# Group norm of a gated linear-attention layer, moved into the scan and counted by tokens

## The chip, the cores and the metric

The kernel runs on one core of one Trainium2 chip. The time is the device time of one whole execution in microseconds (us). Three runs of the kernel before took 2664.95, 2672.15 and 2674.62 us; their median, 2672.15 us, is the time before.

The engines have short names below. PE is TensorE, and PEld its weight load. DVE is VectorE, ACT is ScalarE and POOL is GpSimd. SP is SyncE, which here only issues transfers. Each engine runs its own instructions in program order and waits at semaphores for the others.

## The reference, cut to what matters

The program is a stack of layers on 512 tokens with 1024 features, all in fp32. The change concerns only the end of one layer, an RWKV-7 mixer with 16 heads of 64 features:

```
y = _wkv7_scan(rh, decay, kh, vh, -kk, kk * ah)
mean = jnp.mean(y, axis=-1, keepdims=True)
var = jnp.mean(jnp.square(y - mean), axis=-1, keepdims=True)
y = (y - mean) * lax.rsqrt(var + GN_EPS)
y = y * ln_w.reshape(N_HEADS, HEAD_SIZE) + ln_b.reshape(N_HEADS, HEAD_SIZE)
bonus = jnp.sum(rh * kh * r_k, axis=-1, keepdims=True) * vh
out = ((y + bonus).reshape(bsz, seq, d).astype(h.dtype) * g) @ w_o
```

The scan carries a 64x64 state for each head. Its output y is linear in v. The norm is over the 64 features of a head, for each token. The gate g is `sigmoid(xg @ g1) @ g2`, and g2 (named gw2 in the kernel) and w_o are the two weight matrices that follow the scan.

## The kernel before, in words

**Layout.** Features lie on partitions: a tile [128, 512] is 128 features (two heads) by all 512 tokens, and `YT[:, f]` with f = 0 to 7 is the scan's output. `V[:, f]` is v in the same layout; it later holds the bonus term. `VT` is v with tokens on partitions.

**The scan.** The list `SCAN` is one order of steps, walked by PE, ACT and DVE alike. The tokens are cut into 4 chunks c of 128, each in two halves u of 64. A `group` (c, hf) inverts the in-chunk matrices of four pairs of heads; its steps are pa, px, pk, w and then p, q, t for each level. A `through` (c, u) carries the state over 64 tokens: `at` and `kt` (transposes), `ls` (L times state), `u` (T times that), `y` (the output: `ys` from the state, `yu` from U and v) and `state`. Up to three groups and one through are interleaved. `turn` transposes V into VT, and `bonus` makes the bonus term. After the last group only throughs are left, one behind another: this is called the tail here.

**After the scan.** The list `GROUP_NORM` interleaves four steps over the 8 feature tiles. A matmul with `bones` (ones within a head) spreads each head's sum to its 64 rows. DVE then centres YT. ACT squares it into `g4`, a second matmul with `bones` gives the variance, ACT takes its root, and DVE inverts the whole [128, 512] tile (line 1968), scales (1970) and adds ln_b and the bonus term (1973). Then come the dense products.

**Dense products.** `dense(name, ...)` walks the weight pieces. Each piece goes from `raw_` (4 slots, loaded by SP) into `WHs` by ACT (line 1063, "hi") and the rest into `WLs` by DVE (line 1571, "lo"), with 3 slots for the split pieces and a lookahead of 2 (`AHEAD`). A block of 128 output features takes three matmuls for each 128 input rows (lines 597 to 599). A "k" or "g" piece holds one k for several output blocks, so PE can start with k = 0 alone; an "m" piece holds all k of one block. The input of w_o is YT times the gate's product (DVE, line 1985). It is split by ACT (`oghi`, line 1358) and by DVE (even m, line 1988) or POOL (odd m, line 2277) into `oglo`.

**Banks.** PSUM has 8 banks, given out in turn by `Banks`; a taker waits until the bank's last contents were read ("free"). A held bank is skipped.

**Weights over the scan's memory.** The slots of raw_, WHs and WLs lie over the scan's buffers nb_. SP therefore loads the pieces from `HALT` on (the first of gw2) only when the groups have ended, and ACT splits them only after the last Y.

## Time and profile before

| | us |
|---|---|
| median of three runs | 2672.15 |
| the profiled execution, its own time | 2671.66 |
| its span, first to last instruction | 2669.8 |
| busy: PE, DVE, ACT, POOL | 2512.4, 1383.5, 899.7, 235.2 |
| the scan with what follows it, to the last matmul of w_o | about 805 to 1126.6 |

Starts and durations in the profile are in us from the span's start. A row of the timeline reads: start, duration, engine, line and operation, output<-input, shape, xcount, and in brackets the idle time of the engine just before it and what ended it. One fp32 matmul stands as two MATMUL records, a transpose as one, and a matmul on the split (fp32r) operands as one.

### The profile page before, as it was taken

To read this page: it belongs to the slowest core of one execution; us is meant where nothing else is said; L and a number is where in the kernel's file an instruction comes from. 1 tells how busy PE (TensorE), PEld (TensorE's weight loads), DVE (VectorE), ACT (ScalarE), POOL (GpSimd) and SP (SyncE) were. 2 spreads that over 40 slices of the span, in tenths; PEclk is the share of its full clock that TensorE was granted. 3 is DMA by queue.
4 is the path that set the end of the run, shared out by engine and by line. 5 is a ranking of instruction groups with operands and counts; after the bars stand their busy time and mean duration, and the time that the engine had idled before them with its cause. 6 is when DMAs were issued, how large, how long until landed. Compare 5 with 4: busy or idle time off the path is not lost.

```text
span 2669.8 us, 37239 instructions
## 1 busy us (share of the span) xinstructions
PE 2512.4 (94%) x15944; PEld 2037.9 (76%) x15944; DVE 1383.5 (52%) x2011; ACT 899.7 (34%) x1338; POOL 235.2 (9%) x199
## 2 busy tenths in 40 slices
PE   5999999989897895899999999999999999999998
PEld 4787888866676883688888888888766887788886
DVE  6774756647644547553344544433344654554433
ACT  3222413234642232242243332222245543332221
POOL 0000000002320000000000011100222000011100
PEclk9998999989999997999999999999999999999999
DMA  7563656612210001223332332233211331233332
GB/s 308 171 192 112 194 191 189 189 60 91 71 48 3 4 35 56 71 87 101 95 97 91 92 102 95 91 103 117 79 48 44 116 121 58 89 102 95 96 97 68
DMA packets 77796, 271.64 MB, mean 102 GB/s; under 512 B 8801, under 2 KB 9057, under 8 KB 76865
## 3 DMA queue, kind: packets, MB, share of 16 engines
q1 hardware_dynamic: 65808, 224.79, 26.3%
q0 software_dynamic: 11824, 44.49, 5.2%
q8 instruction: 126, 2.06, 0.3%
q14 instruction: 38, 0.30, 0.0%
HBM read 265.05 MB, written 4.19 MB: 101 GB/s over the span
## 4 chain that ended last, share of the span: by engine, by line
PE 85%; DVE 9%; ACT 3%; issue 2%; DMA 1%; SPq 0%; POOL 0%; DVEq 0%; ACTq 0%
PE ps L597 24%; PE ps L599 24%; PE ps L598 24%; PE ps L613 2%; DVE WLs L1571 2%; ACT WHs L1063 1%; DVE sqa L1968 1%; DMA raw<-in_cw_in_k 1%; PE ps L745 1%; DVE ada L1587 1%; PE ps L735 1%; PE ps L785 1%; PE ps L638 1%; PE ps L1013 1%; PE ps L1027 1%
## 5 line engine op out<-in xcount | busy, mean ns | idle before, releaser
L597 PE MATMUL ps<-HH,WHs 128*128 128x512 f32 x1728 | 695.7, 403 | 23.7 <-DVE HL L1657 11.5
L1571 DVE TENSOR_TENSOR WLs<-raw,WHs 128x1024 fp32r<-128x1024 f32 (+2 forms) x402 | 465.3, 1158 | 438.4 <-ACT WHs L1063 437.8
L599 PE MATMUL ps<-HH,WLs 128*128 128x512 f32 x1728 | 677.4, 392 | 0.0
L598 PE MATMUL ps<-HL,WHs 128*128 128x512 f32 x1728 | 676.9, 392 | 0.0
L1063 ACT ACTIVATE WHs<-raw 128x1024 fp32r<-128x1024 f32 (+2 forms) x420 | 415.6, 991 | 565.6 <-PE ps L599 562.5
L597 PEld LDWEIGHTS ps<-HH,WHs 128*128 128x128 f32 x1728 | 327.3, 189 | 102.3 <-issue 27.3
L599 PEld LDWEIGHTS ps<-HH,WLs 128*128 128x128 f32 x1728 | 326.7, 189 | 69.3
L598 PEld LDWEIGHTS ps<-HL,WHs 128*128 128x128 f32 x1728 | 327.5, 190 | 66.4 <-issue 2.2
L597 PE MATMUL ps<-HM,WHs 128*128 128x512 f32 x576 | 224.1, 389 | 0.0
L598 PE MATMUL ps<-HM,WHs 128*128 128x512 f32 x576 | 224.1, 389 | 0.0
L599 PE MATMUL ps<-HM,WLs 128*128 128x512 f32 x576 | 224.1, 389 | 0.0
L597 PE MATMUL ps<-HID,WHs 128*128 128x512 f32 x352 | 136.9, 389 | 0.0
L598 PE MATMUL ps<-HID,WHs 128*128 128x512 f32 x352 | 136.9, 389 | 0.0
L599 PE MATMUL ps<-HID,WLs 128*128 128x512 f32 x352 | 136.9, 389 | 0.0
L1108 ACT ACTIVATE sqa<-X 128x512 f32<-128x512 f32 x72 | 45.3, 631 | 238.2 <-DVE X L1628 234.8
L599 PEld LDWEIGHTS ps<-HM,WLs 128*128 128x128 f32 x576 | 108.1, 188 | 22.5
L597 PEld LDWEIGHTS ps<-HM,WHs 128*128 128x128 f32 x576 | 108.1, 188 | 22.5
L598 PEld LDWEIGHTS ps<-HM,WHs 128*128 128x128 f32 x576 | 108.1, 188 | 22.3
L2283 POOL TENSOR_TENSOR tmp<-tmp,sqa 128x512 f32<-128x512 f32 x24 | 41.3, 1722 | 868.8 <-ACT sqa L1392 868.8
L1587 DVE CUSTOM_DVE_ANT_0 ada<-ada,cbc 128x1024 f32<-128x1024 f32 x96 | 116.9, 1218 | 0.0
L597 PE MATMUL ps<-M0H,WHs 128*128 128x512 f32 x192 | 81.8, 426 | 29.5 <-DVE WLs L1571 17.6
L1733 DVE TENSOR_TENSOR tmp<-tmp 128x512 f32<-128x512 f32 x64 | 44.2, 691 | 102.6 <-ACT HM L1168 102.5
(371 smaller groups left out, 3222.0 us busy)
## 6 DMA issues: line engine op xcount, KB each, us to landing
ada<-in_adaw POOLq DMA_DIRECT2D x80, 512.0 KB, 4.8
raw<-in_f1gu_m SPq DMA_DIRECT2D x38, 512.0 KB, 3.6
raw<-in_f2gu_m SPq DMA_DIRECT2D x38, 512.0 KB, 3.6
raw<-in_mw_0b SPq DMA_DIRECT2D x32, 512.0 KB, 3.6
raw<-in_mw_1b SPq DMA_DIRECT2D x32, 512.0 KB, 3.6
raw<-in_w_in_m SPq DMA_DIRECT2D x18, 512.0 KB, 3.6
ada<-in_adaw SPq DMA_DIRECT2D x16, 512.0 KB, 15.3
raw<-in_cw_in_m SPq DMA_DIRECT2D x16, 512.0 KB, 3.7
```

What stands on the lines that cost most here:

```text
L597: pe.matmul(o[m], WHs[:, s, w], hi, start=k == 0, stop=False)
L598: pe.matmul(o[m], WHs[:, s, w], lo, start=False, stop=False)
L599: t = pe.matmul(o[m], WLs[:, s, w], hi, start=False, stop=k == DEPTH_K[name] - 1)
L613: t = pe.transpose(o[:, 128 * j:128 * j + 128], x(j), ident[:, :])
L638: t = pe.matmul(o, w[:, 128 * k:128 * k + 128], MW["g"][:, k], start=k == 0, stop=k == 7)
L735: t = pe.matmul(o[half(p), u, 32 * i:32 * i + 32], XT[half(u), n:n + 64], odd(T[half(u), m:m + 64], 2 << lv), start=True, stop=True)
L1063: act.activation(WHs[:, SLOT[v], 0:n], raw_[:, v % NRAW, 0:n], ACT.Copy).then_inc(*S.up("w_hi", ("hi", v)))
L1108: act.activation(sqt[f % 2][:, 0:n], src, ACT.Square).then_inc(*S.up("a_norm", ("sq", tag, f)))
L1571: dve.tensor_tensor(WLs[:, s, 0:n], raw_[:, v % NRAW, 0:n], WHs[:, s, 0:n].bitcast(F32), SUB).then_inc(*S.up("w_lo", ("lo", v)))
L1587: dve.tensor_tensor_reduce(tile, tile, cbc, 1.0, 0.0, MUL, ADD, mod[:, u:u + 1]).then_inc(*S.up("v_mod", ("dot", u)))
L1733: dve.tensor_tensor(x, x, x, MUL).then_inc(*S.up("v_evac", ("t2", name, m)))
L2283: pool.tensor_tensor(a_, a_, sqt[j % 2], MUL).then_inc(*S.up("g_ffn", ("ga", n, j)))
```

## The change

- v is centred per head before the scan: `turn` now multiplies V by `cen` = identity minus bones/64 instead of transposing it. Since y is linear in v, y comes out centred, and the mean step goes.
- The group norm is made per chunk of 128 tokens, in five steps placed in SCAN (chunks 0 to 2) or behind it (chunk 3). `squares`: ACT squares [128, 1024]. `sums`: 8 matmuls with the squares as weights and two columns of bones give a [128, 16] tile with tokens on partitions. `root` is made on that tile by ACT, and its reciprocal by DVE. `spread`: 16 matmuls of a broadcast column with the identity bring it back over two banks. `apply`: three DVE operations on [128, 1024] multiply by it, multiply by ln_w, and add V. ln_b is now added to V beforehand, by 8 ACT operations at the bonus steps (`V3`).
- gw2 is split in the tail (`gate_in`, `gate_weights`), and its 48 matmuls are issued as gate 0 to gate 7 between the steps of the last through and of chunk 3's norm. Each gate holds a bank. The two banks for chunk 3's spread are reserved ahead of gate 0.
- w_o becomes kind "g": eight pieces of one k and four blocks, then four "m" pieces. The products with the gate are made in a loop ahead of `dense("w_o")`. GHs and the state ST move to other places, and the slots are renumbered so that gw2 begins at slot 0.

```
+        ("gw2", "k", 8, 2), ("w_o", "g", 8, 8),
         ("mw1_1a", "e", 16, 8), ("mw2_1a", "m", 8, 16), ("mw1_1b", "m", 16, 8), ("mw2_1b", "m", 8, 16),
...
-EARLIER = {u: SPLIT[i - NSPLIT] for i, u in enumerate(SPLIT) if i >= NSPLIT}
+SLOT = {u: (i - SPLIT.index(HALT)) % NSPLIT for i, u in enumerate(SPLIT)}
+EARLIER = {u: SPLIT[i - NSPLIT] for i, u in enumerate(SPLIT) if i >= NSPLIT and not HALT <= u < HALT + NSPLIT}
 
...
+    for c in range(3):
+        part["norm", c] = [("norm", c, x) for x in ("squares", "sums", "root", "spread", "apply")]
+    part["gate_in"] = [("gate_in",)]
     groups = [("group", c, hf) for c in range(4) for hf in range(2)]
-    throughs = [("through", c, u) for c in range(4) for u in range(2)]
+    throughs = [("through", c, u) for c in range(4) for u in range(2)][:-1]
     at, ended, live, out = dict.fromkeys(part, 0), set(), ["turn", "bonus"], []
...
+                    live.append(("norm", x[1]))
+                if x == ("norm", 2):
+                    live.append("gate_in")
         if not live and not groups and throughs:
             live.append(throughs.pop(0))
-    return out
+    out += [("through", 3, 1, "ls"), ("gate_weights",), ("through", 3, 1, "u"), ("gate", 0), ("through", 3, 1, "y"), ("gate", 1)]
+    for i, x in enumerate(("squares", "sums", "root", "spread", "apply")):
+        out += [("norm", 3, x), ("gate", 2 + i)]
+    return out + [("gate", 7)]
 
...
-        g4 = [sqa[:, i] for i in range(4)]
...
+        gsq = sqa[:, 0:2].rearrange("p a (f t) -> p (a f) t", t=128)
+        pair = lambda c: YT[:, :, 128 * c:128 * c + 128]
...
+            def group_norm(c, part):
+                if part == "sums":
+                    o = bank("gsum", c)
+                    on.wait_ge(*S.at("gsq", c))
+                    for f in range(8):
+                        t = pe.matmul(o[:, 2 * f:2 * f + 2], gsq[:, f], bones[:, 0:128:64], start=True, stop=True)
+                    t.then_inc(*S.up("mm_scan", ("full", "gsum", c)))
+                if part == "spread":
+                    o = taken_two("gn", c) if c == 3 else bank_two("gn", c)
+                    on.wait_ge(*S.at("grec", c))
+                    for f in range(8):
+                        for p in range(2):
+                            n = 16 * c + 2 * f + p
+                            t = pe.matmul(o[half(p), f // 4, 128 * (f % 4):128 * (f % 4) + 128], ur[:, n:n + 1].to_broadcast([128, 64]),
+                                          ident[:, :], start=True, stop=True)
+                    t.then_inc(*S.up("mm_scan", ("full", "gn", c)))
+                    if c == 3:
+                        B.release(("gn", c), 2)
+
+            def gate_out(m):
+                u = FIRST["gw2"]
+                if m == 0:
+                    bank_two("gn", 3, hold=True)
+                o = bank("gw2", m, hold=True)
+                for k in range(2):
+                    on.wait_ge(*S.at("lo", u + k))
+                    on.wait_ge(*S.at("ghlo", k))
+                    s, w = SLOT[u + k], slice(128 * m, 128 * m + 128)
+                    pe.matmul(o, WHs[:, s, w], GHs[:, 0, k], start=k == 0, stop=False)
+                    pe.matmul(o, WHs[:, s, w], GHs[:, 1, k], start=False, stop=False)
+                    t = pe.matmul(o, WLs[:, s, w], GHs[:, 0, k], start=False, stop=k == 1)
+                t.then_inc(*S.up("mm_dense", ("full", "gw2", m), ("used", u), ("used", u + 1)))
+
...
                     for f in range(x[1], x[1] + 4):
                         o = bank("vt", f)
                         on.wait_ge(*S.at("V", f))
-                        turn(o, lambda j: V[:, f, 128 * j:128 * j + 128], [("full", "vt", f)], "mm_scan")
+
+                        for j in range(4):
+                            t = pe.matmul(o[:, 128 * j:128 * j + 128], V[:, f, 128 * j:128 * j + 128], cen[:, :], start=True, stop=True)
+                        t.then_inc(*S.up("mm_scan", ("full", "vt", f)))
                 if x[0] == "bonus":
...
 
-            for row in GROUP_NORM:
-                for f, step in row:
-                    if step == 0:
-                        on.wait_ge(*S.at("Y", 3, 1))
-                        o = bank("mean", f, hold=True)
-                        pe.matmul(o, bones[:, :], YT[:, f], start=True, stop=True).then_inc(*S.up("mm_scan", ("full", "mean", f)))
-                    if step == 1:
-                        B.release(("mean", f))
-                        on.wait_ge(*S.at("gs", f))
-                        o = bank("var", f, hold=True)
-                        pe.matmul(o, bones[:, :], g4[f % 4], start=True, stop=True).then_inc(*S.up("mm_scan", ("full", "var", f)))
-                    if step == 2:
-                        B.release(("var", f))
-
-            dense("gw2", lambda k: (GHs[:, 0, k], GHs[:, 1, k]), lambda k: ("ghlo", k))
...
                     if v == HALT:
-                        on.wait_ge(*S.at("Y", 3, 1))
+                        on.wait_ge(*S.at("full", "w", 3, 1, 1))
+                        on.wait_ge(*S.at("full", "u", 5, 1))
+                    if v == HALT + 2:
+                        on.wait_ge(*S.at("full", "u", 7, 1))
+                        on.wait_ge(*S.at("full", "ys", 7))
...
 
+            def group_norm(c, part):
+                if part == "squares":
+                    if c:
+                        on.wait_ge(*S.at("full", "gsum", c - 1))
+                    else:
+                        on.wait_ge(*S.at("full", "bonus", 7))
+                    on.wait_ge(*S.at("Y", c, 1))
+                    act.activation(gsq, pair(c), ACT.Square).then_inc(*S.up("a_scan", ("gsq", c)))
+                if part == "root":
+                    on.wait_ge(*S.at("full", "gsum", c))
+                    act.activation(ur[:, 16 * c:16 * c + 16], taken("gsum", c)[:, 0:16], ACT.Sqrt, scale=1.0 / 64,
+                                   bias=eps6[:, 1:2]).then_inc(*S.up("a_scan", ("gr", c), ("free", "gsum", c)))
+
             for x in SCAN:
+                if x[0] == "norm":
+                    group_norm(*x[1:])
+                if x == ("gate_in",):
+                    on.wait_ge(*S.at("Y", 2, 1))
+                    for j in range(2):
+                        on.wait_ge(*S.at("gk", j))
+                        act.activation(GHs[:, 0, j], GH[:, j], ACT.Copy).then_inc(*S.up("a_scan", ("ghhi", j)))
+                if x == ("gate_weights",):
+                    ahead(HALT - 1, len(WANT))
+                if x[0] == "bonus" and x[2] == 1:
+                    f = x[1]
+                    on.wait_ge(*S.at("V2", f))
+                    act.activation(V[:, f], V[:, f], ACT.Identity, bias=vc("ln_b", f)).then_inc(*S.up("a_scan", ("V3", f)))
                 if x[0] == "turn":
...
 
-            for n, row in enumerate(GROUP_NORM):
-                for f, step in row:
-                    if step == 1:
-                        on.wait_ge(*S.at("gc", f))
-                        if f >= 4:
-                            on.wait_ge(*S.at("gx", f - 4))
-                        act.activation(g4[f % 4], YT[:, f], ACT.Square).then_inc(*S.up("a_scan", ("gs", f)))
-                    if step == 2:
-                        on.wait_ge(*S.at("full", "var", f))
-                        act.activation(g4[f % 4], taken("var", f), ACT.Sqrt, scale=1.0 / 64,
-                                       bias=eps6[:, 1:2]).then_inc(*S.up("a_scan", ("gr", f), ("free", "var", f)))
-                if n == 4:
-                    on.wait_ge(*S.at("Y", 3, 1))
-                    for j in range(2):
-                        on.wait_ge(*S.at("gk", j))
-                        act.activation(GHs[:, 0, j], GH[:, j], ACT.Copy).then_inc(*S.up("a_scan", ("ghhi", j)))
-                if n == 6:
-                    ahead(HALT, len(WANT))
...
 
+            def group_norm(c, part):
+                if part == "root":
+                    u = ur[:, 16 * c:16 * c + 16]
+                    on.wait_ge(*S.at("gr", c))
+                    dve.reciprocal(u, u).then_inc(*S.up("v_scan", ("grec", c)))
+                if part == "apply":
+                    on.wait_ge(*S.at("full", "gn", c))
+                    x = pair(c)
+                    dve.tensor_tensor(x, x, taken_two("gn", c).rearrange("p a (f t) -> p (a f) t", t=128), MUL).then_inc(
+                        *S.up("v_scan", ("gx", c), ("free", "gn", c)))
+                    on.wait_ge(*S.at("gx", c))
+                    w = vc("ln_w", 0, 8).rearrange("p (f o) -> p f o", o=1).to_broadcast([128, 8, 128])
+                    dve.tensor_tensor(x, x, w, MUL).then_inc(*S.up("v_scan", ("gw", c)))
+                    on.wait_ge(*S.at("gw", c))
+                    on.wait_ge(*S.at("V3", 7))
+                    dve.tensor_tensor(x, x, V[:, :, 128 * c:128 * c + 128], ADD).then_inc(*S.up("v_scan", ("o", c)))
+
             for x in SCAN:
+                if x[0] == "norm":
+                    group_norm(*x[1:])
+                if x == ("gate_in",):
+                    for j in range(2):
+                        on.wait_ge(*S.at("ghhi", j))
+                        dve.tensor_tensor(GHs[:, 1, j], GH[:, j], GHs[:, 0, j].bitcast(F32), SUB).then_inc(*S.up("v_scan", ("ghlo", j)))
+                if x == ("gate_weights",):
+                    ahead(HALT - 1, len(WANT))
                 if x[0] == "bonus":
...
-                        dve.scalar_tensor_tensor(out=YT[:, f], in0=YT[:, f], scalar=vc("ln_b", f), in1=V[:, f], op0=ADD,
-                                                 op1=ADD).then_inc(*S.up("v_scan", ("o", f)))
-                if n == 4:
-                    for j in range(2):
-                        on.wait_ge(*S.at("ghhi", j))
-                        dve.tensor_tensor(GHs[:, 1, j], GH[:, j], GHs[:, 0, j].bitcast(F32), SUB).then_inc(*S.up("v_scan", ("ghlo", j)))
-                if n == 6:
-                    ahead(HALT, len(WANT))
-
...
+            ahead(FIRST["w_o"], len(WANT))
+            for m in range(8):
                 on.wait_ge(*S.at("full", "gw2", m))
-                on.wait_ge(*S.at("o", m))
+                on.wait_ge(*S.at("o", 3))
                 dve.tensor_tensor(YT[:, m], YT[:, m], taken("gw2", m), MUL).then_inc(*S.up("v_evac", ("og", m), ("free", "gw2", m)))
                 if m % 2 == 0:
                     on.wait_ge(*S.at("oghi", m))
                     dve.tensor_tensor(MX[0][1][:, m], YT[:, m], MX[0][0][:, m].bitcast(F32), SUB).then_inc(*S.up("v_in", ("oglo", m)))
-
-            dense("gw2", gate_out)
             dense("w_o", residual("w_o"))
```

## Rows read from the trace of the kernel before

**Rows 1.** Busy time by engine, three stretches (start:end, length, busy, granted clock, DMA)

```profile
940.00:960.00 20.00, 19.52 (x657) 18.85 (x658) 8.68 (x21) 7.39 (x14) 0.00 (x0) 1.00 0.02 4
...
1016.00:1063.00 47.00, 22.20 (x33) 7.15 (x33) 39.80 (x32) 14.89 (x21) 0.00 (x0) 0.71 0.22 78
1063.00:1126.70 63.70, 57.59 (x241) 44.41 (x239) 38.34 (x42) 18.79 (x26) 5.06 (x4) 1.00 0.22 70
```

**Rows 2.** Who waited for whom, 1016 to 1087 (total, times, longest)

```profile
PE ps L848 <- ACT sqa L1343: 24.8, 8, 7.9
```

**Rows 3.** Groups by line, 790 to 1130 (xcount | busy, mean ns | idle before)

```profile
L1968 DVE RECIPROCAL sqa<-sqa 128x512 f32<-128x512 f32 x8 | 26.7, 3343 | 0.0
...
L1571 DVE TENSOR_TENSOR WLs<-raw,WHs 128x1024 fp32r<-128x1024 f32 x13 | 16.0, 1240 | 5.8 <-ACT WHs L1063 5.8
...
L1063 ACT ACTIVATE WHs<-raw 128x1024 fp32r<-128x1024 f32 x12 | 12.3, 1043 | 5.0 <-PE ps L599 5.0
...
L1970 DVE SCALAR_TENSOR_TENSOR VY<-VY,vec,sqa 128x512 f32<-128x512 f32 x8 | 6.0, 752 | 0.3
```

**Rows 4.** Timeline, from the last Y to the end of w_o

```profile
1015.28 0.69 DVE L1926 TENSOR_TENSOR VY<-VY,ps 128x512 f32<-128x512 f32 x1 [2.88 <-PE ps L803]
...
1018.59 1.12 PE L848 MATMUL ps<-sqa,bones 128*128 128x512 f32 x2 [1.45 <-ACT sqa L1343]
...
1056.84 2.07 PE L848 MATMUL ps<-sqa,bones 128*128 128x512 f32 x2 [7.87 <-ACT sqa L1343]
...
1062.84 0.79 PE L597 MATMUL ps<-GHs,WHs 128*128 128x512 f32 x1
...
1074.50 0.47 PE L597 MATMUL ps<-M0H,WHs 128*128 128x512 f32 x1
...
1126.23 0.40 PE L599 MATMUL ps<-M0H,WLs 128*128 128x512 f32 x1
```

**Rows 5.** Timeline, the loop of gate products and their splits

```profile
1072.28 0.68 DVE L1985 TENSOR_TENSOR VY<-VY,ps 128x512 f32<-128x512 f32 x1
...
1074.27 1.28 DVE L1985 TENSOR_TENSOR VY<-VY,ps 128x512 f32<-128x512 f32 x2
...
1075.69 1.26 POOL L2277 TENSOR_TENSOR M0L<-VY,M0H 128x512 fp32r<-128x512 f32 x1 [288.95 <-ACT M0H L1358]
...
1076.24 1.26 DVE L1988 TENSOR_TENSOR M0L<-VY,M0H 128x512 fp32r<-128x512 f32 x1 [0.69 <-ACT M0H L1358]
...
1077.43 1.27 DVE L1985 TENSOR_TENSOR VY<-VY,ps 128x512 f32<-128x512 f32 x2
```

**Rows 6.** Timeline of the tail: chunk 3's first through

```profile
991.95 2.93 PE L613 MATMUL ps<-ident,KVA 128*128 128x128 f32 x16
...
994.80 1.76 PE L772 MATMUL ps<-nb,LR 64*64 64x64 f32 x32
...
997.35 2.02 PE L785 MATMUL ps<-nb,X 64*64 64x64 f32 x31 [0.79 <-DVE nb L1917]
...
1002.43 0.69 DVE L1926 TENSOR_TENSOR VY<-VY,ps 128x512 f32<-128x512 f32 x1 [2.28 <-PE ps L803]
...
1004.30 0.69 DVE L1934 TENSOR_TENSOR nb<-nb,ps 128x512 f32<-128x512 f32 x1 [1.18 <-PE ps L816]
...
1008.00 3.35 PE L785 MATMUL ps<-nb,X 64*64 64x64 f32 x29 [0.78 <-DVE nb L1917]
```

**Rows 7.** Timeline: the nearest relatives of `spread`, of `sums`, and a transpose

```profile
751.72 1.09 PE L676 MATMUL ps<-ident,ur 128*64 128x128 f32 x16
...
756.77 3.40 PE L668 MATMUL ps<-bones,sqa 128*128 128x2 f32 x29
...
804.92 1.91 PE L613 MATMUL ps<-ident,KVA 128*128 128x128 f32 x16
```

**Rows 8.** Table loads of ACT, by line, 900 to 1400

```profile
L1346 ACT ACT_TABLE_LOAD x1 | 1.3, 1283 | 0.0
```

**Rows 9.** Transfers, 975 to 1130 (KB each, median us from issue to landing)

```profile
X<-x_keep SPq DMA_DIRECT2D x1, 2048.0 KB, 8.0
```

66 lines of the change are left out of this document (23 added, 43 removed), and 1 row of the table PROJ.

## The prediction

> **What bounds the kernel now.** I read the page first: PE is busy for 94% of the span, so the kernel gains only where PE stands idle, or where its work is taken away. The busy time by stretches shows the one weak place near the change. From 1016 to 1063 PE is busy for 22.2 of 47 us, at a granted clock of 0.71, while DVE is busy for 39.8 [rows 1]. This is the group norm. Before it, at 940 to 960, PE is busy for 19.5 of 20 us; after it the clock is 1.00 again [rows 1]. The waits name what PE lacked: in eight matmuls it waited 24.8 us for ACT's squares, 7.9 us at the longest [rows 2]. ACT in turn stood behind DVE. The groups by line show why: eight reciprocals of [128, 512] cost 3.34 us each, 26.7 us, with no idle time before them, and the scale and the ln_b step add two times 0.75 for each tile [rows 3]. So DVE sets the order of the 47 us. The timeline gives the frame of my sum: the last Y ends at 1015.97, the gate's product begins at 1062.84 and w_o at 1074.50, and the last matmul of w_o ends at 1126.63 [rows 4]. What follows w_o is the same in both kernels, so the end of w_o carries the difference.
>
> **Rates.** 48 gate matmuls take 1074.50 - 1062.84 = 11.66 us [rows 4]; the first is slow, the others come every 0.235 us. Six (one gate) cost 1.4, twelve (one k of four blocks) 2.8, 24 (one block of w_o) 5.6. The nearest row to `spread` has 8 such matmuls (16 records) in 1.09 us [rows 7], so 16 cost 2.1. The nearest to `sums` has 29 records in 3.40, or 0.117 each [rows 7]; 16 records cost 1.85. DVE on [128, 1024] takes 1.24 and ACT 1.04 [rows 3]; I halve these for 512 columns: 0.6 to 0.65.
>
> **Work added before the last Y.**
>
> Centring v. A transpose costs 1.91/16 = 0.12 [rows 7]. A product with `cen` is two records of 0.117, or 0.23. For 32 of them that is 3.8 us more; a DVE wait can hide part of the second half. I take 3.2 (bounds 1 and 7). A rule of the Trainium skill speaks more strongly against this edit: "TensorE: Matmul & The Clock Gate", Terms, has fp32 transposes four times faster through the transpose mode. By it a product would cost 0.48 and the edit 11.5 us; the rows, where ordinary fp32 products of that weight size come every 0.23, don't bear that out.
>
> Norms 0 and 1 lie among the groups. PE is nearly full there [rows 1], so its share, 1.85 + 2.1 = 3.95 each, goes on the path: 7.9. DVE's `apply` is 3 x 1.24 = 3.7 and blocks masks and additions queued behind it. DVE is busy for only 8.7 of 20 us [rows 1], and three groups are in flight, so I count 0.8 for each norm beside that. Sum 9.5; lower bound 5, if PE's share fills idle time; upper bound 24, if nothing is hidden (12 each: 3.95 + 3.7, 1.1 for the squares, 1.3 for a table load, some 2 of semaphores). The square root's table load, 1.28 us once [rows 8], moves into norm 0. It runs on ACT beside p3's matmuls and costs nothing; uncovered, it would be 1.3. The eight ln_b additions on ACT (5 us) wait for DVE's V2, but ACT's next moves need PE steps that come later: nothing, 5 if uncovered.
>
> Norm 2 lies in the tail, where one through's steps wait for each other. `sums` stands between at and kt: 1.85 on the path. `spread` stands ahead of u. Before, PE waited there 0.8 us for DVE [rows 6], so 2.1 costs 1.3. `apply` (3.7) stands on DVE ahead of the Y addition; DVE idles 2.28 and then 1.18 there [rows 6], 3.46 in all, so 0.25 stays. Together 3.0 after a little overlap (3.4 at most). The split of GH and of gw2's two pieces (DVE 1.3 + 2.5) lies beside ls (1.76) and u (3.35) [rows 6] and costs nothing; without u's slow clock, 1. `sums` and `spread` wait for nobody late.
>
> Gate 0 stands between u and the last y: 1.4. All further gates lie beside waits.
>
> The last Y moves from 1015.97 by 3.2 + 9.5 + 3.0 + 1.4 = 17.1 to 1033.1. Call it t0.
>
> **From t0 to w_o.** Gate 1 begins before t0, gate 2 follows, and both end at t0 + 2.05, after ACT's square (1.1). Sums to 3.9, gate 3 to 5.3, gate 4 to 6.7, while root and reciprocal of 16 columns run beside them; spread to 8.8. DVE's first multiplication ends at 10.15. Only that frees the two banks of the spread, and following the bank turns gate 5 takes the first of them. So gates 5 to 7 run from 10.2 to 14.4. Now a wait that the order adds: ahead of its loop of gate products DVE walks the weights of w_o to the third piece, and the second's slot is gw2's, free when gate 7 ends. ACT splits at 15.1, DVE at 15.8 and once more at 16.45. All eight gate products, and apply before them, are queued in front of or behind that wait, so the loop begins at t0 + 16.45.
>
> **The loop and w_o.** The loop keeps its pace: the first product at 1072.28, pairs at 1074.27 and 1077.43, so 2.0 for the first and 3.15 for each pair; DVE's 1.26 lies beside POOL's 1.26 [rows 5]. Eight products end 12.1 after its start. PE can't use k = 0 at once. By the bank turns, block 0 of w_o takes the bank of gate 3 and block 1 that of gate 4, freed at about 5.8 and 6.4. Three k steps then end at 5.85 + 8.4 = 14.25. The fourth piece of w_o is split only when ACT and DVE have left the loop: 12.1 + 0.7 + 0.6 + 0.65 = 14.1. Both limits agree; five more k steps (14.0) and four blocks (22.4) give 50.65. Before, this part was 1126.63 - 1072.28 = 54.4 from the loop's start, so kind "g" itself brings only some 4 us.
>
> PE stands idle for 7.9 us ahead of w_o. After an idle of 7.87 two records took 2.07, against 1.12 after 1.45, and u in the tail took 3.35 instead of 2.02 [rows 4, 6]. That is the lower clock level, 1.2 GHz, for a while. I add 1.5 (0 to 4).
>
> X's return (8.0 us for 2 MB [rows 9]) is issued at t0, and its first reader comes some 45 us later; w_o's third and fourth piece are queued on SP behind it, and are needed at t0 + 15: nothing, 3 if they are late. The added table `cen` is one 64 KB transfer at the start: nothing.
>
> Sum: w_o ends at 1033.1 + 16.45 + 50.65 + 1.5 = 1101.7 instead of 1126.6, 24.9 us earlier. Against the profiled execution's own 2671.66, which is 0.5 from the median of the runs, that is 2646.8; I say 2647.
>
> **Rivals.**
>
> More is gained (0.10). The norms' PE work fills idle slots (5 instead of 9.5), centring costs 1, and the clock stays up in tail and w_o (3): about 34 to 37 us, 2636. Against it: PE is full where norm 1 lies.
>
> The scan pays for the norms (0.15). An in-order engine that waits for a norm holds up three groups. DVE's reciprocal waits for ACT's root, which is queued behind ACT's moves and a table load; masks stand behind it. At 12 us for each norm, three cost 36 instead of 12.5: 23.5 more, 2670, within 0.5% of before. The 47 us would then only have been moved. For it: the tail has no other work to hide behind. Against it: DVE is less than half busy in the scan.
>
> PE falls to its lower level in w_o (0.05), the slower side. The gate's product, broken into pieces by waits, leaves PE cold, and waits for banks and pieces keep it there. 192 matmuls at twice 0.235 cost 45 more: 2692. It decides from 38 us on, so from most of w_o. Against it: before, w_o began with waits for POOL as well, and the clock there was 1.00 [rows 1]. The Trainium skill ("TensorE: Matmul & The Clock Gate", A second HAM failure mode: psum-queue depth-cycling) tells of micro-idles between groups of matmuls that re-throttle the engine; no row here shows that for dense products.
>
> **Chances and range.** The forecast has 0.70 (its own range 2639 to 2657). A measurement of this kernel can tell about 0.5%, 13.4 us, from no change. Faster by more: 0.70 + 0.10 = 0.80; within: 0.15; slower: 0.05. The range 2634 to 2661 takes in the better rival and the bounds of centring, clock and part of the norms' upper bound.
>
> **What would show it.** The last Y near 1033; no reciprocal of 3.34 us; `sums` near 1.85 and `spread` near 2.1 us; the two-bank multiplication near 1.25; gates 5 to 7 behind that multiplication; DVE waiting about 2 us for ACT's split after gate 7; a first w_o matmul about 22 us after the last Y; the last one near 1102. The prediction is wrong if the groups' stretch grows by over 20 us, if the tail's through stalls at the spread, or if w_o's k steps take over 3 us.

## The result, and the profile after

| us | before | after |
|---|---|---|
| median (7 runs each) | 2672.15 | 2649.41 |
| lowest and highest run | 2663.83, 2674.62 | 2641.63, 2657.82 |
| the profiled execution, its own time | 2671.66 | 2657.82 |
| its span | 2669.8 | 2656.0 |

The ratio is 0.993, with a 95% interval of 0.9909 to 0.9952: 13 to 24 us faster, by the ratio 18.7; by the two medians it is 22.7. The forecast was 2647, or 24.9 us faster. The profiled execution of after is the slowest of its seven runs, so a second profile of the same kernel (e1_again below: 2652.62 us) stands beside it where a size matters.

The page of the changed kernel begins:

```profile
span 2656.0 us, 37616 instructions
...
PE 2524.0 (95%) x16136; PEld 2064.7 (78%) x16136; DVE 1355.3 (51%) x1999; ACT 901.1 (34%) x1342; POOL 235.6 (9%) x200
```

DVE lost 28 us of work and PE gained 12. The groups by line, 790 to 1130, show the new norm's parts (xcount | busy, mean ns | idle before):

```profile
L827 PE MATMUL ps<-ident,ur 128*64 128x128 f32 x128 | 9.3, 307 | 0.0
...
L819 PE MATMUL ps<-bones,sqa 128*128 128x2 f32 x64 | 9.1, 273 | 0.0
...
L858 PE MATMUL ps<-cen,KVA 128*128 128x128 f32 x64 | 7.6, 277 | 0.0
...
L1980 DVE TENSOR_TENSOR VY<-VY,ps 128x1024 f32<-128x1024 f32 x4 | 4.8, 1211 | 4.2 <-PE ps L827 4.2
...
L1976 DVE RECIPROCAL ur<-ur 128x16 f32<-128x16 f32 x4 | 1.0, 252 | 19.0 <-ACT ur L1363 19.0
```

The reciprocals fell from 26.7 us [rows 3] to 1.0. For all four chunks, sums take 9.1 us of PE (L819), the spread 9.3 (L827). Centring takes 7.6 (L858), or 0.24 for each of the 32 products.

Now the milestones, each read from the timeline. The scan is counted from the start of DVE's last `LR<-ps,X` evacuation ahead of it, so that what an execution lost earlier doesn't enter.

| us | before | after | e1_again |
|---|---|---|---|
| start of the scan, to the end of the last Y | 210.9 | 238.3 | 232.0 |
| last Y to the loop of gate products | 56.3 | 16.3 | 16.3 |
| loop's start to the end of w_o | 54.4 | 53.2 | 53.4 |
| start of the scan to the end of w_o | 321.5 | 307.9 | 301.7 |
| end of w_o, absolute | 1126.6 | 1108.8 | 1103.5 |

Behind the last Y 41 us went, and 21 to 27 came back ahead of it. The timeline of after, first inside the scan (chunk 1's norm), then in the tail, then behind the last Y (1038.47):

```profile
975.87 0.25 DVE L1976 RECIPROCAL ur<-ur 128x16 f32<-128x16 f32 x1 [4.12 <-ACT ur L1363]
...
976.96 1.97 PE L827 MATMUL ps<-ident,ur 128*64 128x128 f32 x32
...
980.97 0.68 DVE L1952 COPY sqa<-ps 64x512 f32<-64x512 f32 x1 [3.01 <-PE ps L780]
...
982.37 1.21 DVE L1980 TENSOR_TENSOR VY<-VY,ps 128x1024 f32<-128x1024 f32 x1
...
983.63 1.25 PE L788 MATMUL ps<-LR,nb 64*64 64x64 f32 x32 [1.79 <-DVE VY L1980]
...
1008.72 3.41 PE L819 MATMUL ps<-bones,sqa 128*128 128x2 f32 x16
...
1032.33 0.79 PE L842 MATMUL ps<-GHs,WHs 128*128 128x512 f32 x1
...
1038.47 0.69 DVE L1958 TENSOR_TENSOR VY<-VY,ps 128x512 f32<-128x512 f32 x1 [5.34 <-PE ps L798]
...
1041.22 1.84 PE L819 MATMUL ps<-bones,sqa 128*128 128x2 f32 x16
...
1045.88 1.97 PE L827 MATMUL ps<-ident,ur 128*64 128x128 f32 x32
...
1049.17 0.50 PE L842 MATMUL ps<-GHs,WHs 128*128 128x512 f32 x1 [1.32 <-DVE VY L1980]
...
1054.30 1.29 DVE L1603 TENSOR_TENSOR WLs<-raw,WHs 128x512 fp32r<-128x512 f32 x2 [2.07 <-ACT WHs L1089]
1055.51 0.68 DVE L2020 TENSOR_TENSOR VY<-VY,ps 128x512 f32<-128x512 f32 x1
...
1061.43 0.77 PE L592 MATMUL ps<-M0H,WHs 128*128 128x512 f32 x1 [7.88 <-DVE VY L2020]
```

The reader is to see two things. Everything behind 1038.47 comes as forecast: sums 1.84, spread 1.97, gate 5 at 1049.17 only when DVE's two-bank multiplication is done, DVE's 2.07 us wait at L1603, the loop at 1055.51, and w_o at 1061.43 after 7.88 us of idle PE. Inside the scan, at 983.63, PE waits 1.79 us for that same multiplication. The forecast has no such wait. The list of waits, 805 to 1040, has it twice (total, times, longest):

```profile
PE ps L788 <- DVE VY L1980: 1.8, 1, 1.8
PE ps L608 <- DVE VY L1980: 1.8, 1, 1.8
```

What waits is a taker of one of the spread's two banks: a transpose (L608) in chunk 0's norm, and the output `ys` (L788) in chunk 1's. The spread ends at 978.9, but DVE multiplies only at 982.37: between them stand PE's u (L780), the copy of it (980.97) and four additions of a group, which the common order puts ahead of `apply`. The banks' turn had come round by then.

Busy time by stretches of after (start:end, length, busy, granted clock, DMA):

```profile
965.00:1004.00 39.00, 37.21 (x943) 35.65 (x942) 16.77 (x35) 10.08 (x18) 0.00 (x0) 0.82 0.09 31
...
982.00:984.00 2.00, 0.37 (x12) 0.38 (x14) 1.97 (x5) 0.00 (x0) 0.00 (x0) 1.00 0.03 8
984.00:1000.00 16.00, 16.00 (x348) 15.50 (x343) 6.98 (x13) 2.62 (x5) 0.00 (x0) 0.57 0.01 2
1000.00:1004.00 4.00, 4.00 (x129) 3.95 (x127) 1.03 (x2) 1.53 (x3) 0.00 (x0) 1.00 0.82 281
```

Behind the wait the granted clock is 0.57 for 16 us in which PE is never idle: mostly the lower of its two levels, 1.2 GHz. In the tail it is low for a while too: sums take 3.41 instead of 1.84 (1008.72).

What the lower level costs the scan as a whole is read from the whole stretch, from the start of the scan to the end of the last Y: after, then e3_no_norms (below), the same kernel without the norms of chunks 0 to 2.

```profile
800.84:1039.16 238.32, 209.82 (x5705) 191.68 (x5704) 117.86 (x245) 71.25 (x122) 0.00 (x0) 0.89 0.03 10
```

```profile
802.57:1013.34 210.77, 186.19 (x5561) 169.64 (x5560) 107.06 (x233) 65.79 (x115) 0.00 (x0) 0.94 0.03 11
```

PE is idle for 28.5 us in the first and 24.6 in the second. The three norms' own 144 records come to 11.4 us at full clock (1.84 and 1.97 for each norm), but PE is busy for 23.6 us more. The rest of that is the same work done at the lower level.

### The profile page after: what moved, and what is told of

It is laid out like the page before. It is cut to its first block, busy times and chain, and to the rows that moved or that the text cites. A ratio compares the mean times of both kernels' runs of the same rounds, so it can differ in the third digit from the quotient of the medians.

```text
span 2656.0 us, 37616 instructions
## 1 busy us (share of the span) xinstructions
PE 2524.0 (95%) x16136; PEld 2064.7 (78%) x16136; DVE 1355.3 (51%) x1999; ACT 901.1 (34%) x1342; POOL 235.6 (9%) x200
## 3 DMA queue, kind: packets, MB, share of 16 engines
q1 hardware_dynamic: 66384, 224.79, 25.8%
## 4 chain that ended last, share of the span: by engine, by line
PE 87%; DVE 8%; ACT 3%; issue 1%; DMA 1%; SPq 0%; DVEq 0%; ACTq 0%
PE ps L592 24%; PE ps L593 24%; PE ps L594 24%; PE ps L608 2%; DVE WLs L1603 2%; ACT WHs L1089 1%; PE ps L730 1%; DMA raw<-in_cw_in_k 1%; DVE ada L1619 1%; PE ps L780 1%; PE ps L740 1%; PE ps L633 1%; PE ps L1035 1%; PE ps L1049 1%; PE ps L697 0%
## 5 line engine op out<-in xcount | busy, mean ns | idle before, releaser
L592 PE MATMUL ps<-HH,WHs 128*128 128x512 f32 x1728 | 696.2, 403 | 23.6 <-DVE HL L1689 11.3
L1603 DVE TENSOR_TENSOR WLs<-raw,WHs 128x1024 fp32r<-128x1024 f32 (+2 forms) x406 | 466.4, 1149 | 445.8 <-ACT WHs L1089 445.1
L592 PEld LDWEIGHTS ps<-HH,WHs 128*128 128x128 f32 x1728 | 327.5, 190 | 101.9 <-issue 26.7
L594 PEld LDWEIGHTS ps<-HH,WLs 128*128 128x128 f32 x1728 | 327.2, 189 | 69.8
```

The costliest lines, as they stand in the source:

```text
L592: pe.matmul(o[m], WHs[:, s, w], hi, start=k == 0, stop=False)
L594: t = pe.matmul(o[m], WLs[:, s, w], hi, start=False, stop=k == DEPTH_K[name] - 1)
L1603: dve.tensor_tensor(WLs[:, s, 0:n], raw_[:, v % NRAW, 0:n], WHs[:, s, 0:n].bitcast(F32), SUB).then_inc(*S.up("w_lo", ("lo", v)))
```

## The experiments

e1 to e4 ran on one chip, e5 to e8 on a second, g1 to g4 on a third, each time beside the kernel before. Ratios are to the kernel before on that chip. "Scan" is the first row of the table above, "behind" is the last Y to the end of w_o. "Idle" is what PE did not fill of the scan, and "clock" the granted clock over it, both from one profile by stretches.

| | median us | ratio, interval | scan | idle | clock | behind |
|---|---|---|---|---|---|---|
| e1_again | 2653.32 | 0.9942, 0.9926 to 0.9957 | 232.0 | 26.7 | 0.90 | 69.7 |
| e2_transposed_v | 2648.90 | 0.9928, 0.9910 to 0.9947 | 229.5 | 30.1 | 0.92 | 69.7 |
| e3_no_norms | 2629.54 | 0.9850, 0.9833 to 0.9868 | 210.8 | 24.6 | 0.94 | 69.7 |
| e4_norms_behind | 2645.94 | 0.9916, 0.9892 to 0.9941 | 204.4 | 24.2 | 0.97 | 89.1 |
| e5_gates_behind | 2650.46 | 0.9932, 0.9915 to 0.9950 | 228.6 | 29.3 | 0.92 | 74.6 |
| e6_w_o_blocks | 2653.06 | 0.9936, 0.9921 to 0.9952 | 232.9 | 25.7 | 0.90 | 72.2 |
| e7_weights_late | 2649.58 | 0.9922, 0.9905 to 0.9940 | 233.6 | 27.7 | 0.91 | 68.8 |
| e8_late_banks | 2647.71 | 0.9919, 0.9902 to 0.9936 | 227.7 | 25.8 | 0.92 | 66.5 |
| g1_multiply_early | 2647.65 | 0.9909, 0.9884 to 0.9933 | 226.0 | 26.6 | 0.93 | 69.8 |
| g2_small_apply | 2646.21 | 0.9905, 0.9879 to 0.9931 | 232.5 | 28.1 | 0.91 | 70.0 |
| g3_sums_twice | 2658.23 | 0.9950, 0.9936 to 0.9963 | 237.5 | 26.3 | 0.91 | 69.9 |
| g4_spread_behind | 2633.71 | 0.9858, 0.9830 to 0.9886 | 218.8 | 24.8 | 0.93 | 66.4 |

The same numbers are 210.9, 30.1 and 0.94 for the kernel before, and 238.3, 28.5 and 0.89 for after. A scan of one profile scatters. Five profiles have the changed kernel's steps there (after, e1, e6, e7, e8) and gave 227.7 to 238.3; e3 and e4, which have the same steps ahead of the last Y, gave 210.8 and 204.4. PE's idle time scatters less, 25.7 to 28.5 in the five. "Behind" repeats within 0.4 us where nothing of it was changed. So differences behind the last Y are read from the profile, and those inside the scan from the medians as well.

**e1_again.** The changed kernel as it is, as a yardstick on the chip of e2 to e4.

> The changed kernel once more, unchanged. In its first profile the stretch from the end of wr's last product to the last Y took 27 us longer than before, where the sum had 17.1, and the granted clock in 805 to 1000 was 0.90 against 0.95 before. Theory A (the excess is the clock, which varies between executions): this profile shows another stretch, 222 to 232 us at a clock of 0.93 or more, and the same 16.4 and 53 us behind the last Y. Rival B (the norm's steps cost what they cost, whatever the clock): again 236 to 239 us. Time against before: 0.990 to 0.995 in both.

15 us faster by the ratio (11 to 20). The scan of 232.0 is the upper end of theory A's range, with a clock of 0.92 from 805 to 1000 where it wanted 0.93; the stretches behind the last Y repeat. Both waits for L1980 are there again (1.7 and 1.8 us), and behind the second the clock falls again:

```profile
978.00:996.00 18.00, 16.21 (x347) 15.60 (x341) 8.54 (x15) 2.38 (x4) 0.00 (x0) 0.54 0.01 3
```

**e2_transposed_v.** V is transposed as before and not centred, so the output lacks the mean step:

```
-    for j in range(4):
-        t = pe.matmul(o[:, 128 * j:128 * j + 128], V[:, f, 128 * j:128 * j + 128], cen[:, :], start=True, stop=True)
-    t.then_inc(*S.up("mm_scan", ("full", "vt", f)))
+    turn(o, lambda j: V[:, f, 128 * j:128 * j + 128], [("full", "vt", f)], "mm_scan")
```

> v is turned by plain transposes as before the change; the centring is left out, so y is not centred. Only the 32 products with cen differ. Theory A (a product costs 0.23 us, a transpose 0.12): 3 to 4 us less than the changed kernel, all of it within the first 20 us of the scan. Rival B (hidden behind DVE, which sets the pace there): within 1 us of it.

Scan 2.5 us shorter, medians 4.4 apart, intervals overlapping: these tell no cost. PE's first half did shrink as priced, from 3.73 us (e1_again) to this:

```profile
803.60 1.91 PE L608 MATMUL ps<-ident,KVA 128*128 128x128 f32 x16
```

The cost can be told early in the scan, where all profiles are still in step. DVE's first product of V with a bonus sum (`KVA<-KVA,ps`) begins 9.17 us after the scan's start here, 9.16 in the kernel before, and 10.89 or 10.90 in all twelve profiles with centring: it costs 1.7 us there. Here first, then e1_again:

```profile
812.97 0.68 DVE L2008 TENSOR_TENSOR KVA<-KVA,ps 128x512 f32<-128x512 f32 x1
```

```profile
812.71 0.68 DVE L2010 TENSOR_TENSOR KVA<-KVA,ps 128x512 f32<-128x512 f32 x1
```

Part of PE's added work fills its own waits: over the scan it is idle for 30.1 us here, as before the change, and for 26.7 in e1_again. What is left of the 1.7 us at the end can't be told: the first Y of chunk 0 already comes 102.4 us after the start here, and 101.8 with centring. The forecast's 3.2 was too much; its bounds of 1 and 7 hold.

**e3_no_norms.** Norms 0 to 2 are left out (tokens 0 to 383 stay unnormalized); chunk 3's stays:

```
-                if x[0] == "through" and x[2] == 1:
-                    live.append(("norm", x[1]))
-                if x == ("norm", 2):
+                if x == ("through", 2, 1):
                     live.append("gate_in")
```

> The norm of chunks 0 to 2 is left out altogether (384 tokens stay without it); chunk 3's norm and the gates are as in the changed kernel. Theory A (as predicted, 9.5 us for norms 0 and 1 and 3.0 for norm 2): 12.5 us less than the changed kernel. Rival B (in-order waits behind roots, reciprocals and apply): 20 to 36 us less. Rival C (mostly in idle time): under 7 us less. The last Y comes earlier by the same amount.

The medians differ from e1_again by 23.8 us, the scans by 21.2: rival B by the number. The forecast had 9.5 + 3.0 = 12.5 for the same thing. Of the 21.2, PE's idle time is only 2.1, and 19.1 are busy time, 11.4 of them the norms' own records and some 8 the lower level. In-order waits, rival B's mechanism, would have shown as idle time. The scan without the norms takes 210.8, as before (210.9), though centring and gate 0 are in it. Where chunk 1's norm was, the clock is whole:

```profile
958.00:986.00 28.00, 27.30 (x891) 26.18 (x888) 12.75 (x31) 8.87 (x16) 0.00 (x0) 1.00 0.11 38
```

These 28 us are 39 in e1_again for the same matmuls and a norm's 3.9.

**e4_norms_behind.** All four norms behind the last Y, their steps staggered over the chunks, the gates placed between them:

```
+    parts = ("squares", "sums", "root", "spread", "apply")
+    for r in range(8):
+        out += [("norm", c, parts[r - c]) for c in range(4) if 0 <= r - c < 5]
+        out += {0: [("gate", 2)], 6: [("gate", 3), ("gate", 4), ("gate", 5)], 7: [("gate", 6), ("gate", 7)]}.get(r, [])
```

> All four norms stand behind the last Y, pipelined chunk behind chunk (squares of one beside sums of the one before), with gates 3 to 7 behind the last spread; nothing is left out. PE's 3.95 us for each of three norms moves from the scan to the stretch behind it, where DVE's apply (3.7 us each) runs beside PE. Theory A (the gain is from the norm's smaller tile, not from its place): 0 to 6 us slower than the changed kernel, still 12 or more faster than before. Rival B (the place in the scan carries the gain): 12 to 20 us slower than the changed kernel, so within 8 us of before. If the norms cost the scan over 16 us, it could even be faster than the changed kernel.

Behind the last Y it takes 19.4 us more than e1_again, and ahead of it 27.6 less. It is 7.4 us faster by the medians, with intervals that overlap: neither theory, but the case named last in the expectation. So the norm's place in the scan brought nothing that can be told: three norms cost 19 us behind it, where PE waits and stands at its lower level for part of them, and 21 to 24 inside it. The timeline behind the last Y (1003.0):

```profile
1011.63 3.68 PE L827 MATMUL ps<-ident,ur 128*64 128x128 f32 x32 [1.31 <-ACT ur L1363]
...
1043.37 0.56 PE L592 MATMUL ps<-M0H,WHs 128*128 128x512 f32 x1 [4.74 <-DVE VY L2020]
```

**e5_gates_behind.** Gates 0 to 7 all behind chunk 3's norm, none between its steps; the spread's banks are then not reserved:

```
+    out += [("through", 3, 1, "ls"), ("gate_weights",), ("through", 3, 1, "u"), ("through", 3, 1, "y")]
+    out += [("norm", 3, x) for x in ("squares", "sums", "root", "spread", "apply")]
+    return out + [("gate", m) for m in range(8)]
...
```

> All eight gates stand behind chunk 3's norm instead of between the steps of the last through and of the norm; nothing is left out. Theory A: gate 0 leaves the path before the last Y (1.4 us, 2.9 at the lower clock), and behind it 11.3 us of matmuls begin at the spread's end, 5.6 us after the last Y, so gate 7 ends 16.9 us after it instead of 14.4: 0 to 2 us slower than the changed kernel, perhaps faster. Rival B (filling PE's idle time is what brings the gain and keeps the clock up): 6 to 10 us slower.

Behind 74.6 instead of 69.7, but gates 0 and 1 no longer stand ahead of the last Y. Start of the scan to the end of w_o is 303.2 against 301.7, and the scan alone scatters by more than that, so no cost of giving up the interleaving can be told; the 6 to 10 us of rival B aren't there. Chunk 3's norm now has only itself to run, and runs slowly:

```profile
1029.93 3.57 PE L818 MATMUL ps<-bones,sqa 128*128 128x2 f32 x16 [1.87 <-ACT sqa L1355]
...
1034.16 3.68 PE L826 MATMUL ps<-ident,ur 128*64 128x128 f32 x32 [0.65 <-DVE ur L1971]
```

In this kernel both waits for the two-bank multiplication occur (1.7 and 1.8 us, line 1975 here), yet the stretch with chunk 1's norm is at full clock; the tail is at 0.72 instead:

```profile
961.00:994.00 33.00, 30.52 (x917) 29.14 (x919) 16.43 (x34) 9.98 (x18) 0.00 (x0) 1.00 0.08 25
994.00:1029.00 35.00, 29.79 (x521) 28.48 (x517) 15.99 (x21) 10.38 (x17) 0.00 (x0) 0.72 0.08 27
```

**e6_w_o_blocks.** w_o in eight "m" pieces again, as before the change: `("w_o", "m", 8, 8)` for `("w_o", "g", 8, 8)`, with its array cut to match.

> w_o stays in pieces of one output block with all k, as before the change; everything else as in the changed kernel. Theory A: the one-k pieces bring some 4 us, since before the first block waited for every k: 3 to 5 us slower than the changed kernel. Rival B: the DVE loop of 12.1 us sets the start of all but the first blocks in both, and the fourth small piece waits for the loop: within 1.5 us.

Behind 72.2: kind "g" is worth 2.5 us here, between the two theories; the forecast had 4. PE waits longer ahead of w_o, and once more inside it, 1.48 us for POOL's half of the split at 1067.35:

```profile
1059.03 0.77 PE L592 MATMUL ps<-M0H,WHs 128*128 128x512 f32 x1 [9.38 <-DVE VY L2020]
```

**e7_weights_late and e8_late_banks.** e7 splits w_o's second and third piece inside the loop of gate products, not ahead of it. e8 adds that block m of w_o takes gate m's bank:

```
-            ahead(FIRST["w_o"], len(WANT))
+            ahead(FIRST["w_o"] - 2, len(WANT))
             for m in range(8):
+                if m in (4, 6):
+                    ahead(FIRST["w_o"] + (m - 4) // 2, len(WANT))
...
+                            if name == "w_o" and m < 4:
+                                B.turn = B.place["gw2", m]
```

> ACT and DVE split only the first piece of w_o ahead of the loop of gate products; the second and third are split inside the loop before product 4, the fourth before product 6. Nothing is left out. Theory A: the loop starts at 13.3 instead of 16.4 us after the last Y, since it no longer waits for gate 7, and w_o ends 3.2 us earlier. Rival B: the splits inside the loop delay the products, and the gain is under 1 us.

> As the kernel with the late weights, and the first four blocks of w_o take the banks of gates 0, 1, 2, 3 in that order instead of 3, 4, 1, 2. Nothing is left out. Theory A: the first matmul of w_o no longer waits for the fourth and fifth gate product; PE starts 2 to 4 us after the loop does instead of 5.9, and w_o ends 2 us earlier than with late weights alone, 5 us earlier than in the changed kernel. Rival B: the products for later k set the pace anyway, and it equals the kernel with late weights.

In e7 the loop starts 3.3 us earlier (13.0 behind the last Y) and w_o ends only 0.9 earlier: its first matmul still comes 5.9 us after the loop's start, for the banks. In e8 that is 2.2, and w_o ends 3.2 earlier:

```profile
1043.88 0.47 PE L594 MATMUL ps<-M0H,WHs 128*128 128x512 f32 x1 [0.83 <-DVE M0L L2029]
```

So the two waits that the forecast named were there, DVE's for gate 7 and w_o's for the banks of gates 3 and 4. Taking away the first alone mostly brings out the second; the second alone wasn't taken away. Together they were worth 3.2 us, where the expectation had 5.

**g1_multiply_early.** DVE's first multiplication is walked right behind `spread`, not with `apply`. It does the same work and frees the two banks earlier:

```
-                if part == "apply":
+                if part == "spread":
                     on.wait_ge(*S.at("full", "gn", c))
...
+                if part == "apply":
+                    x = pair(c)
                     on.wait_ge(*S.at("gx", c))
```

> The same operations; only DVE's first multiplication of each norm, which frees the two banks of the spread, stands directly behind the spread in DVE's order instead of one step later. In all profiles of the changed kernel PE waited 1.8 us for it in norm 1 and 1.7 to 1.8 us in norm 0, when the through's and the turn's matmuls came to those banks. Theory A (the bank turn is part of the excess, and the waits bring the lower clock after them): both waits go, the scan is 3 to 8 us shorter than its 228 to 238 us, and the clock in norm 1's stretch is nearer 1.00 than 0.80. Rival B (the spread's PE time alone is the cost): the waits move elsewhere (DVE then waits for the spread, and masks stand behind it), and the scan stays at 228 or more.

Neither wait for L1980 inside the scan is left. The multiplication stands ahead of the copy now, and the clock of the stretch is 0.95 (0.78 in e1_again, 0.82 in after). Timeline, then the stretch:

```profile
974.13 1.22 DVE L1980 TENSOR_TENSOR VY<-VY,ps 128x1024 f32<-128x1024 f32 x1 [0.86 <-PE ps L827]
976.12 0.68 DVE L1952 COPY sqa<-ps 64x512 f32<-64x512 f32 x1 [0.78 <-PE ps L780]
```

```profile
959.00:992.00 33.00, 32.30 (x943) 30.94 (x943) 16.70 (x35) 10.30 (x18) 0.00 (x0) 0.95 0.10 35
992.00:1028.00 36.00, 31.77 (x505) 29.31 (x499) 15.20 (x21) 10.20 (x16) 0.00 (x0) 0.72 0.05 17
```

The scan takes 226.0, 6 us less than e1_again, but only 1.7 less than the shortest of the five profiles of the changed order (e8, 227.7). PE's idle time didn't shrink: 26.6 us against 26.7. The two waits are gone, and other waits of the same sum stand elsewhere, as rival B had it. All 6 us are busy time, 205.3 in e1_again and 199.4 here. So what went in this profile is time at the lower level. The ratio is 0.0033 below e1_again's (8.8 us), on another chip and with intervals that overlap a little; against after's, 0.993, it is 0.0021. A gain is likely, and its size isn't shown.

One fall of the clock is left in this stretch, and it has no wait ahead of it:

```profile
957.00:967.40 10.40, 10.40 (x290) 9.87 (x287) 3.68 (x9) 4.31 (x8) 0.00 (x0) 1.00 0.02 5
967.40:970.90 3.50, 3.50 (x38) 3.17 (x37) 0.25 (x1) 2.50 (x5) 0.00 (x0) 0.51 0.00 0
970.90:983.00 12.10, 12.10 (x393) 11.65 (x393) 7.61 (x14) 2.86 (x5) 0.00 (x0) 1.00 0.02 4
```

PE was busy without a gap, and what it did last ahead of the fall was norm 1's sums (964.87 to 966.8), 16 matmuls of two columns. The same fall, right behind these sums and with no idle time in the 8 us before, stands in the profiles of e2, e6, e8 and g2.

**g2_small_apply.** For chunks 0 to 2, DVE reads 16 columns of the spread in place of the multiplication of [128, 1024], so tokens 0 to 383 are left unscaled by the root:

```
+                if part == "apply" and c < 3:
+                    on.wait_ge(*S.at("full", "gn", c))
+                    dve.tensor_copy(lmid[:, 0:2, :], taken_two("gn", c)[:, :, 0:8]).then_inc(*S.up("v_scan", ("gx", c), ("free", "gn", c)))
```

> DVE's three [128, 1024] operations of norms 0 to 2 are replaced by one copy of 16 columns that frees the banks; these 384 tokens stay unscaled. PE's and ACT's norm work stays. Without any norm for these chunks the scan took 210.8 us, with all of it 228 to 238. Theory A (PE's 11.9 us is the main cost, DVE's share comes through bank waits and clock): 223 to 226 us. Rival B (DVE blocked by apply is the main cost): 216 or less. Rival C (DVE's share costs nothing): 228 or more.

Both waits are there, at 0.7 us each: the same bank turns, shorter by what DVE no longer does (1.2 us). The scan is 232.5, as e1_again's, so by its number rival C holds. DVE is busy for 107.5 us of it instead of 117.6, and PE's idle time is 28.1, no less than in the changed kernel: DVE's share of the three norms cost the scan nothing that can be told. Its median is 1.4 us from g1's. Less DVE work and the same work done earlier can't be told apart.

**g3_sums_twice.** Chunks 0 to 2 compute their sums twice (`for f in list(range(8)) * (2 if c < 3 else 1)`); the result is the same.

> The eight two-column matmuls of sums are issued twice for chunks 0 to 2; the second pass writes the same values. PE work grows by 3 x 1.85 = 5.6 us. Theory A (they cost their time): the scan is 5 to 7 us longer than the changed kernel's 232. Rival B (two-column matmuls leave the engine nearly empty and draw the lower clock): over 10 us longer, with a granted clock below 0.9 directly behind the sums. Rival C (hidden): under 3 us.

The scan takes 237.5, 5.5 more than e1_again, where 48 more records of 0.117 make 5.6: theory A by the number. That the two agree so well is luck, since the scan scatters by 10 us. And the rate wasn't that of the row: norm 1's 32 records took 5.43 us instead of 3.7.

```profile
966.91 5.43 PE L819 MATMUL ps<-bones,sqa 128*128 128x2 f32 x32
```

The clock fell in the midst of them, though PE had been busy without a gap:

```profile
960.00:966.90 6.90, 6.90 (x233) 6.38 (x229) 3.08 (x7) 3.26 (x6) 0.00 (x0) 1.00 0.01 2
966.90:968.60 1.70, 1.70 (x21) 1.69 (x16) 0.61 (x3) 0.00 (x0) 0.00 (x0) 1.00 0.04 10
968.60:975.60 7.00, 7.00 (x35) 6.85 (x34) 0.00 (x0) 1.76 (x3) 0.00 (x0) 0.51 0.00 0
```

With single sums such a fall lasts 3.4 us (g1), with double ones 6.8. That is rival B's mechanism, at less than its price. By the medians it is 10.6 us behind g1, on the same chip and with intervals apart: these 5.6, and what g1's earlier multiplication is worth.

**g4_spread_behind.** Everything is computed. Norms 0 to 2 keep squares, sums and root among the groups; their spreads and applies go into the last through and behind it, where PE waits for DVE. It has the edits of e8 too:

```
-        part["norm", c] = [("norm", c, x) for x in ("squares", "sums", "root", "spread", "apply")]
+        part["norm", c] = [("norm", c, x) for x in ("squares", "sums", "root")]
...
+    out += [("through", 3, 1, "ls"), ("gate_weights",), ("through", 3, 1, "u"), ("norm", 0, "spread"), ("norm", 0, "apply"),
+            ("through", 3, 1, "y"), ("norm", 1, "spread"), ("norm", 3, "squares"), ("norm", 1, "apply"), ("norm", 2, "spread"),
+            ("norm", 3, "sums"), ("norm", 3, "root"), ("norm", 2, "apply"), ("gate", 0), ("norm", 3, "spread"), ("norm", 3, "apply")]
+    return out + [("gate", m) for m in range(1, 8)]
```

> The version that the runs so far point to, nothing left out: squares, sums and root of chunks 0 to 2 stay in the scan; spread and apply of chunk 0 stand between u and y of the last through, those of chunks 1 and 2 behind the last y beside chunk 3's own chain, then the gates; w_o's weights are split late, its first blocks take banks 0 to 3 of the gates. Theory A (spread and apply cost more inside the scan than behind it): the scan takes about 217 us, from the last Y to the end of w_o 63 to 66, so 281 us from the scan's start against 294 to 308 in the changed kernel's versions; 0.984 to 0.988 of the time before. Rival B (behind the scan DVE becomes the bound again and PE goes cold): 290 us or more, equal to the norms-behind kernel at 0.992.

It is the fastest that computes all: 38 us below the kernel before by the medians of its chip, and 14 below g1. Scan and "behind" sum to 285.2 us, between theory A's 281 and rival B's 290, and the ratio is A's. e8's edits, 3.2 us, are in it too. Its stretches, from the groups' last on:

```profile
957.00:986.00 29.00, 28.31 (x889) 27.25 (x890) 12.77 (x31) 9.98 (x18) 0.00 (x0) 1.00 0.09 31
986.00:1017.00 31.00, 27.92 (x527) 26.51 (x523) 15.75 (x21) 10.10 (x16) 0.00 (x0) 0.78 0.09 28
1017.00:1035.00 18.00, 18.00 (x158) 15.49 (x153) 15.05 (x17) 3.71 (x6) 1.06 (x1) 1.00 0.44 162
```

The first stretch is e3's without norms (28 us) plus one, though norm 1's sums stand in it. Behind the last Y (1017) PE is busy for 18.0 of 18 us, at full clock, where after has 13.22 of 22. One price shows in the tail: a spread at the lower level takes 3.68.

```profile
1009.35 3.68 PE L829 MATMUL ps<-ident,ur 128*64 128x128 f32 x32
```

## Why the prediction came out right, point by point

**What bounds.** Right: the 47 us of DVE's norm behind the last Y [rows 1, 3] are what went. Last Y to the loop fell from 56.3 to 16.3.

**Centring v, 3.2.** Too high, inside its bounds. PE's price was right (0.24 a product), but part of it lies in PE's waits for DVE: 1.7 us are left 11 us into the scan, and no more can be told at its end (e2). The rule of the Trainium skill that was weighed there ("TensorE: Matmul & The Clock Gate", Terms), a factor of four, would have made it 11.5; the trace doesn't agree (1.91 against 3.73 for the same half, a factor of two).

**Norms 0 and 1: 9.5, norm 2: 3.0.** This is the mis-sized term. e3 measures 24 us by the medians and 21 in the scan, inside the bound given (24 for two norms) but twice the value taken. The forecast's own items were near: it had 11 us of PE work, and the records come to 11.4; it had 1.9 for what DVE holds up, and PE's idle time grew by 2.1. What it put at nothing in the scan is the clock. The same work took some 8 us longer in e1_again than in e3, and 12 in after, because PE stood at its lower level for longer.

Two things stand ahead of these stretches in the traces. One is the wait of 1.8 us for the spread's banks. The forecast followed the bank turns behind the last Y and not inside the scan, where the multiplication stands behind a group's additions in DVE's order. Eight profiles have this wait in norm 1, and in seven of them (all but e5) 10 to 17 us at the lower level follow it. The other is the sums themselves: in six of the eleven profiles that have norm 1's sums in the scan the clock falls at them or right behind, with no idle time before (g1, g3). From 130 to 185 us into the scan, where norm 1 stands, the clock is 1.00 throughout in before, e3 and e4, which have no norm there. So in this stretch the lower level comes with the norms. What decides in which execution, and how it divides between waits and sums, isn't shown; and in the tail the clock is low without norms too (0.81 in e3).

**Gate 0, 1.4.** It took 2.85 us in after (1032.33 to 1035.18), PE being at its lower level behind the tail's waits. It is within the scatter of the scan.

**Last Y at 1033.1.** It ended at 1039.2 in after and at 1033.8 in e1_again: +27.4 and +21.1 from the start of the scan, forecast +17.1. That the second comes so near is luck: the scan began at 805.1 before, 800.8 in after and 801.8 in e1_again, and over the profiles of the changed versions this start scatters from 798.6 to 804.0.

**From the last Y to the loop, 16.45.** Measured 16.3, by the steps named: both ends of the gates, the two-bank multiplication (1.22), gates 5 to 7 behind it, DVE's 2.07 us wait for ACT's split.

**The loop and w_o, 50.65 + 1.5.** Measured 53.2 and 53.4; first matmul of w_o after 5.9 (5.8), behind an idle of 7.88 (7.9). Kind "g" brought 2.5, not 4. The clock of the stretch is 0.90 in after.

**The sum.** Behind the last Y 69.6 against 68.6. The miss lies in the scan: from its start to the end of w_o 13.6 us were gained in after and 19.8 in e1_again, forecast 24.9. The absolute end of w_o, 1108.8 and 1103.5 instead of 1101.7, and the median, 2.4 us from the forecast, look better than that. In part this is luck: the earlier start of the scan, and the scatter of the executions; by the ratio 18.7 us were gained.

**The rivals.** "The scan pays for the norms" was half right: 8 us for each norm instead of 12, and by another mechanism. Not an in-order engine's queue but the clock took it. With 12 each the kernel would be where it was. The lower level in w_o didn't last beyond its first matmuls (to 1066.4 in after, 5 us). "More is gained" didn't occur in this kernel; its sum, 34 to 37 us, is what g4 reaches by another order.

**Open.** What makes PE's level fall in one execution's scan and not in another's. Whether sums with other shapes would leave the clock alone. Whether the spread's cost in the groups' stretch could vanish with other banks alone wasn't tried.

## What to carry to other kernels

Follow the turn of the buffers at every place where a moved step takes one, not only at the end: a two-bank result whose reader stands far down its engine's queue holds up the next taker. A step moved onto the bounding engine costs its full time wherever it is full; it is cheap only beside that engine's own waits, as in the last through and behind it. Then split a stretch's growth into PE's idle time and its busy time beyond the added records: here most of the unforeseen cost was the second, the clock, and the list of waits alone would have hidden it. Here the gain came from the norm's form (16 columns of reciprocals for 512), while its place in the scan brought nothing that can be told.

## What the runs showed of the hardware

A two-column matmul with 128 weight columns isn't cheap. 16 records take 1.84 us at 2.4 GHz (0.115 each), about as much as a record of centring, which has 128 columns and the same size of weights (0.117), while `spread`, with 64 weight columns and 128 on the other side, takes 0.062 a record (1.97 us for 32). So in these three forms the pace goes with the weights' columns. At 1.2 GHz the sums take 3.57 us and the spread 3.68, about double.

In two profiles of the changed kernel PE's granted clock stood at 0.57 and 0.54 for 16 and 18 us behind a wait of 1.8 us, in a stretch where PE had been busy all along; in e5 it didn't. In g1 and g3 it fell to 0.51 at the two-column sums or right behind them, with PE busy for 10.4 and 8.6 us without a gap before.

Executions of the same kernel lie up to 16 us apart, and the granted clock moves with them: 0.978 in after's run of 2641.63 us, 0.971 in that of 2657.82.
